# The end of a second down projection: six rounds tile by tile instead of two, and the last rows added and stored in halves

## What is computed

```python
def _swiglu(x, w_in, w_out):
    gate, up = jnp.split(x @ w_in, 2, axis=-1)
    return (jax.nn.silu(gate) * up) @ w_out
...
        x = x + _rms_norm(mix, g[1])
        ff = _swiglu(_rms_norm(x, g[2]), ffn_in_w[layer], ffn_out_w[layer])
        x = x + _rms_norm(ff, g[3])
    return x
```

## Time and profile before

| what | value |
|---|---|
| median of 3 runs | 2276.36 us |
| lowest, highest | 2276.23, 2277.83 us |
| the profiled execution | 2276.5 us |
| its span, first to last instruction | 2274.7 us |
| mean granted TensorE clock | 0.996 |
| TensorE matmuls, busy | 2216.5 us (97%) |
| VectorE busy | 1688.2 us (74%) |
| ScalarE busy | 961.8 us (42%) |
| GpSimd busy | 485.3 us (21%) |

### The profile page before, as it was taken

How to read it: one execution, slowest core, us unless ns; L and a number is a source line. 1 busy time by engine, 2 the same in 40 slices (tenths; PEclk the granted TensorE clock), 3 DMA queues, 4 the chain that set the end, 5 groups by cost and what they waited for, 6 DMA issues and landing times. The chain is left out here.

```text
span 2274.7 us, 31865 instructions
## 1 busy us (share of the span) xinstructions
PE 2216.5 (97%) x10604; PEld 1849.1 (81%) x10604; DVE 1688.2 (74%) x2529; ACT 961.8 (42%) x1758; POOL 485.3 (21%) x416
## 2 busy tenths in 40 slices
PE   7999998999999999999999999999899999999998
PEld 6888787888888888877888888888788888888886
DVE  6988768777777667797767666676877777776768
ACT  4322255322222243564556656565532222223453
POOL 5000025333232101252110011002533333310113
PEclk9999999999999999999999999999999999999999
DMA  5122242333333487635333333234133333338764
GB/s 158 37 56 56 71 173 63 98 114 95 111 98 111 139 274 242 215 116 167 84 85 76 68 79 76 59 112 144 47 116 102 107 102 107 102 107 281 246 227 171
DMA packets 246010, 278.24 MB, mean 122 GB/s; under 512 B 18528, under 2 KB 157792, under 8 KB 243808
## 3 DMA queue, kind: packets, MB, share of 16 engines
q1 hardware_dynamic: 242656, 264.84, 38.0%
q10 hardware_dynamic: 3200, 11.54, 1.5%
HBM read 202.40 MB, written 48.76 MB: 110 GB/s over the span
## 5 line engine op out<-in xcount | busy, mean ns | idle before, releaser
L1249 PE MATMUL banks<-xb_mid,up_split 128*128 128x512 f32 x2064 | 475.8, 389 | 2.2 <-DVE up_split L2380 2.2
L1249 PEld LDWEIGHTS banks<-xb_mid,up_split 128*128 128x128 f32 x2064 | 387.1, 188 | 82.9 <-DVE up_split L2380 2.6
L1338 PE MATMUL banks<-down_split 128*128 128x512 f32 x1848 | 423.0, 390 | 4.5 <-DVE down_split L2747 3.2
L1338 PEld LDWEIGHTS banks<-down_split 128*128 128x128 f32 x1848 | 345.4, 188 | 80.7 <-DVE down_split L2747 7.8
L1249 PE MATMUL banks<-xb_low,up_split 128*128 128x512 f32 x1584 | 370.1, 392 | 4.3 <-issue 2.0
L1249 PEld LDWEIGHTS banks<-xb_low,up_split 128*128 128x128 f32 x1584 | 299.3, 189 | 67.7 <-DVE up_split L2380 3.1
L2747 DVE TENSOR_TENSOR down_split<-down_raw,down_split 128x1024 fp32r<-128x1024 f32 x154 | 199.3, 1294 | 107.2 <-ACT down_split L1954 106.9
L1954 ACT CAST down_split<-down_raw 128x1024 fp32r<-128x1024 f32 x154 | 162.0, 1052 | 203.9 <-PE banks L1338 166.2
L3389 POOL TENSOR_TENSOR sums<-raw_up 128x512 f32<-128x512 f32 x88 | 117.5, 1339 | 482.1 <-DMA raw_up<-in_ffn_in_w 261.9
L1383 PE MATMUL banks<-x_hi,w_second 128*128 128x512 f32 x672 | 176.3, 394 | 0.0
L3060 DVE CUSTOM_DVE_ANT_0 scores<-banks,bias 128x896 f32<-128x896 f32 (+7 forms) x128 | 96.7, 756 | 79.3 <-PE banks L1420 63.6
(11 more groups left out here) (227 smaller groups left out, 3607.1 us busy)
## 6 DMA issues: line engine op xcount, KB each, us to landing
raw_up<-in_ffn_in_w SPq DMA_DIRECT2D x88, 512.0 KB, 5.0
down_raw<-in_ffn_out_w SPq DMA_DIRECT2D x154, 256.0 KB, 3.4
down_raw<-hid_spill SPq DMA_DIRECT2D x154, 256.0 KB, 4.1
hid_spill<-hid_mix SPq DMA_DIRECT2D x110, 256.0 KB, 4.8
down_second<-in_ffn_out_w SPq DMA_DIRECT2D x66, 256.0 KB, 3.3
k_stack<-k_parts SPq DMA_DIRECT2D x32, 512.0 KB, 6.3
hid_spill<-hid SPq DMA_DIRECT2D x44, 256.0 KB, 2.0
raw_up<-in_conv_in_w SPq DMA_DIRECT2D x18, 512.0 KB, 5.2
```

The source lines that it names most:

```text
L1249: mm = pe.matmul(bank(b_out), up_part(ph, p, a)[:, q * P:(q + 1) * P], block(RIGHT_OF[p], b)[:, q, :], start=(i == 0), stop=(i == len(pass ...
L1338: mm = pe.matmul(bank(b_out), side[:, a, 0, i * P:(i + 1) * P], side[:, b, 1, :], start=(p in (M3, M5, M1, M2) and first and j == 0), stop ...
```

## The change

It does four things, in `down1` alone.

- The splits of the last six rounds (71 to 76) go to six slots of their own (`down_last`, 48 KB), so `split_high` no longer waits for `down_done` in these rounds.
- TensorE makes the last six rounds tile by tile: tile 0's matmuls of rounds 71 to 76, 18 in all, then tile 1's, and so on. Within tile 0 it waits for each round's split when it comes to it.
- VectorE's order in the tail is one tile after the other: sum, gain, and the addition in two halves of 512 columns, each with a signal (`end_done`). The last tile's gain goes to a tile of its own (`last_gained`) and waits for the sum, not for the square.
- SyncE stores each of the rows 4 to 7 as two transfers of 256 KB, each when its half is added.

```diff
+BY_TILE = {"down0": 2, "down1": 6}
...
+        down_last = at(48, "down_last", [BY_TILE["down1"], 2, 2, HALF], F32R)
+        last_gained = at(8, "last_gained", [HALF])
...
+        end_done = signal("end_done", norm4=2 * HT)
...
         def down_part(ph, q):
 
+            if ph == "down1" and q >= QN - BY_TILE[ph]:
+                return down_last[:, q - (QN - BY_TILE[ph])]
             return down_split[:, DOWN_SLOTS[ph][q % DOWN_RING]]
...
-            for t in range(TT):
-                if t < HT:
-                    sp.wait_ge(*x_new.at("norm4", t + 1))
+            for t in range(HT):
+                sp.wait_ge(*x_new.at("norm4", t + 1))
                 sp.wait_ge(*x_new_right.at("norm4", t + 1))
                 sp.dma_start(out[0, t * P:(t + 1) * P, :], resid[:, t, :]).then_inc(stored, 16)
-            sp.wait_ge(stored, 16 * TT)
+            for t in range(HT, TT):
+                for j in range(2):
+                    sp.wait_ge(*end_done.at("norm4", 2 * (t - HT) + j + 1))
+                    sp.dma_start(out[0, t * P:(t + 1) * P, j * HALF:(j + 1) * HALF],
+                                 resid[:, t, j * HALF:(j + 1) * HALF]).then_inc(stored, 16)
+            sp.wait_ge(stored, 16 * (TT + HT))
...
-                    if i == HT - 1 and q < QN - 2:
+                    if i == HT - 1 and q < QN - BY_TILE[ph]:
                         mm.then_inc(down_done.sem, 1)
                     elif i == HT - 1 and q == QN - 1:
-                        mm.then_inc(down_done.sem, 2)
+                        mm.then_inc(down_done.sem, BY_TILE[ph])
...
-                for q in range(QN - 2):
+                for q in range(QN - BY_TILE[ph]):
...
-                pe.wait_ge(*down_lo.at(ph, 2 * QN))
                 for i in range(HT):
-                    for q in range(QN - 2, QN):
+                    for q in range(QN - BY_TILE[ph], QN):
+                        if i == 0:
+                            pe.wait_ge(*down_lo.at(ph, 2 * (q + 1)))
                         tile_product(q, i)
...
-                else:
+                elif q < QN - BY_TILE[ph] or ph == "down0":
                     act.wait_ge(*down_done.at(ph, q - DOWN_RING + 1))
...
+                def end_added(i, halves):
+
+                    t = HT + i
+                    dve.wait_ge(*rstd1_done.at(norm_ph, t + 1))
+                    dve.wait_ge(*mix_done.at(ph, t + 1))
+                    for j in halves:
+                        part = resid[:, t, j * HALF:(j + 1) * HALF]
+                        gained = last_gained[:] if j and i == HT - 1 else acc_half(t, j)
+                        dve.scalar_tensor_tensor(out=part, in0=gained, scalar=rstd1[:, t:t + 1], in1=part,
+                                                 op0=ALU.mult, op1=ALU.add).then_inc(end_done.sem, 1)
+
+                if not pre:
+                    for i in range(HT):
+                        sum_c22(i)
+                        if i == HT - 1:
+                            dve.wait_ge(*left_gained.at(ph, i + 1))
+                            dve.wait_ge(*c22_sum.at(ph, i + 1))
+                            dve.tensor_tensor(last_gained[:], acc_half(HT + i, 1), g_post[:, HALF:], ALU.mult) \
+                               .then_inc(mix_done.sem, 1)
+                        else:
+                            gain_right(i)
+                        end_added(i, (0, 1))
+                    return
```

More of the change, by code:

```diff
@@ L2227, in _ @@
             grant(dve, lo_ready, u_done, tap_done, ymul_done, yl_done, mix_first, mix_done, x_new_right,
-                  up_lo, u2_done, u3_done, c22_done, c21_done, c12_done, c11_done,
+                  up_lo, u2_done, u3_done, c22_done, c21_done, c12_done, c11_done, end_done,
                   v_sum_done, hid1_done, hid2_done, mix_made,
```

## The result

The changed kernel takes 2281.6 us, the median of 22 runs (2278.73 to 2283.07); the kernel before took 2276.93 on the same chip (22 runs). The ratio is **1.0017, 95% interval 1.0011 to 1.0023**, or +2.5 to +5.2 us. That is slower, and just inside the 0.2% that counts as no change; the two medians alone are 4.67 us apart (1.0021), just outside it. The forecast was 2281.0 us. The profiled execution took 2282.74 us, 1.14 more than the median.

What follows compares the result with a forecast made beforehand. VectorE was taken to pace the splits at the end of down1, with the tail behind TensorE. Starved tile +7.03, shorter tail -3.77 (net +3.26), lag +0.5, clock +0.85: +4.6 us, 2281.0 us; range 2279.2 to 2283.0.

Steps and rivals of the forecast that it cites:

- The likeliest case: End of down1: tile 0 starved of splits and TensorE's clock falling; +4.6 us, 2281.0 us, chance 0.72.
- round 76 ready, from the first matmul of round 71: End of down1: TensorE gets the last split at 2258.30, 0.45 us earlier than before.
- 57 matmuls to the sum of tile 3, at full clock: TensorE behind the last split: 57 matmuls of 0.2267 us plus 0.32, tile 3 summed at 2271.54; +7.03 us.
- clock: TensorE at the end of down1: waits between short groups lower its clock; +0.85 us, between 0 and 1.5.
- VectorE's lag: VectorE's chain in tiles 0 to 2: mean collides with gain, next sum at 4.32 not 4.08; up to +0.72, taken +0.5 us.
- last sum to the end: Tail from tile 3's sum to the span's end: 6.42 us instead of 10.19.
- VectorE paces the splits: End of down1: VectorE's block sums and low parts, not the ring of three slots, set the pace; TensorE fed just in time.
- 57 instead of 24 matmuls behind the last split: TensorE, end of down1: tile 0 needs all six splits first, so 57 matmuls are left at round 76; +7.03 us.
- The tail: After tile 3's sum: tiles further apart, an idle GpSimd and half-row stores shorten it; -3.77 us.
- No collision on VectorE: Rival, splits of down1: low parts take 1.21 us each, round 76 ready 2.2 us sooner; +2.4, 2278.8 us, chance 0.05.
- The splits run ahead: Rival, down1: the ring held the splits, own slots free them; -3.9 us, 2272.5 us, not slower; chance 0.03.

Runs made afterwards that it cites:

- experiment 3: The change with 23 unread matmuls added in TensorE's waits of tile 0; 2279.26 us, ratio 1.0011 to the kernel before.
- experiment 4: The change with every tile's gain, not the last's alone, in a tile of its own ahead of the square; 2279.49 us, ratio 1.0012 to before.
- experiment 2: The change with GpSimd's gains of the left halves of tiles 2 and 3 held until the last low part; 2279.91 us, ratio 1.0013 to before.
- experiment 12: Repeat: the change with four rounds tile by tile, GpSimd's gains and stores held, early gains, additions one tile behind sums; 2273.71 us, ratio 0.9985 to before.
- Experiment 1: The change with before's tail (sums in before's order, whole last rows added and stored at once); 2282.17 us, ratio 1.0024 to before.
- experiment 6: The change with GpSimd's gains and the stores of rows 0 to 3 held until the last low part, every gain early; 2279.07 us, ratio 1.0008 to before.

## Why the prediction was right, step by step

The likeliest case came, a starved first tile and a fall of the clock. The class was left open, 0.52 for slower and 0.47 for no change, and the ratio of 1.0017 falls to the second. Term by term (us of the stretch):

| step of the prediction | forecast | profile after |
|---|---|---|
| round 76 ready, from the first matmul of round 71 | 2258.30 - 2247.74 = 10.56 | 10.53 |
| 57 matmuls to the sum of tile 3, at full clock | 57 x 0.2267 + 0.32 = 13.24 | 13.22 (experiment 3) + 0.04 (experiment 4) = 13.26 |
| clock | 0.85 | 14.21 - 13.22 = 0.99 |
| VectorE's lag | 0.5 | 0.48 - 0.04 = 0.44 |
| last sum to the end | 6.42 | 6.32 |
| all | 31.57 | 31.54 |

That the sum agrees to 0.03 is partly luck: the clock term was taken between 0 and 1.5, and the profile is of one execution.

- *VectorE paces the splits.* The windows of after are full, as the earlier trace rows were, which alone is no proof; experiment 2 shows it: with shorter low parts the split came sooner, until VectorE stood waiting for a load. The slots of their own bought 0.48 us (11.01 to 10.53), the wait of the earlier trace rows. Beyond that, ScalarE's wait for TensorE was no brake there.
- *57 instead of 24 matmuls behind the last split.* Shown by the groups of three in the timeline, and by 39 in experiment 12.
- *The tail.* Experiment 1 puts the change with its own tail 2.2 us below the change with before's, at nearly the same distance of the tiles. The last addition's end to the span's end took 2280.9 - 2278.48 = 2.42, with the lower end for the landing taken (2.48).
- *The lag.* The collision of the mean with the gain was read from the earlier trace rows alone, and it came: 0.75, the sums 4.40 and 4.30 apart. With the clock up (experiment 3) the lag was 0.69, against the full 0.72. So the slowed TensorE did hide a part.
- *The clock.* The fall came, as in the earlier trace rows and not as in the earlier trace rows, but no wait as long as the 2.01 us of the earlier trace rows stood before it: the waits were 1.00 and 0.77, with three matmuls between them. The Trainium skill, page "TensorE: Matmul & The Clock Gate", section "HAM oscillation — how this bites in real kernels", says that matmuls in bursts shorter than the waits between them start at the lowered clock each time. The trace agrees in that the clock is at 0.50 from about 2251.8 to 2262, but the waits of the page's example are longer than any here. The prediction put one fall at up to 1.5 us. The 57 matmuls show a price of 1.0 in the change, 1.6 in experiment 2 and 1.4 in 6. Experiments 1 and 4 have the change's own TensorE work and order up to there, and show 0.87 and 0.33: so even with the same work it is not one number. What differs is how long the clock stays low behind the last split, by windows of 1 us: 2.1 us in the change, 0.8 in experiment 4, and 3.4 in experiment 2, where the clock had risen and fell a second time. About half of that is the price.

One price among the rivals was wrong. *No collision on VectorE* took round 76 as 2.2 us sooner with short low parts. Experiment 2 made them short and won 0.34 (10.53 to 10.19): the next supplier, the loads, was only that far behind. With the stores held as well the round came 9.19 us after the stretch begins (experiment 6), so the 3.4 that *The splits run ahead* asks for was out of reach of every kernel here.

What stays open: whether the loads of rounds 72 to 76 could come sooner by another order of the queue, which was not tried; what the holds and the additions one tile behind the sums are each worth to four rounds; and why a profile's upstream part varies by microseconds.

## What to carry to other kernels

When an accumulation ends tile by tile, count the matmuls left when the last operand comes: k rounds of T tiles are T x k groups of matmuls, tile 0 can have done k - 1 of them (here 24 - 5 = 19 groups of three, 57 matmuls), and all the rest is behind the slowest supplier. Few rounds make the tail the bound, many starve the first tile; here three and four had the shortest stretches, and they were run only with the holds and with the additions one tile behind the sums. Before pricing the removal of a wait, look for the next supplier's distance: it was 0.34 us here, not 2.2.

## What the runs showed of the hardware that was not expected

- The first matmul of round 71 began between 2245.80 and 2249.38 us in 14 profiles, although the edits touch only what lies at the program's end; a difference of two spans can hold 3.6 us that no edit made. Runs of the kernel before alone lie between 2275.91 and 2281.56.
- TensorE's clock fell after two waits of only 1.00 and 0.77 us with a group of three matmuls between them; with 23 unread matmuls put into these waits it stayed at 1.00 (experiment 3).
- With the four stores of finished rows issued 0.53 us behind it, the last hidden block of 256 KB was used 5.49 us after its issue, and VectorE had waited 1.80 for it (experiment 2). With these stores held (experiment 6) it was used 4.50 us after its issue without a wait; the block before it cost a wait of 0.61.
